# An eighteenth pair of experts' rows in seven products, and the sums added back in two passes instead of four

## What is computed

```
u     = take(expert_down, idx)                    # the picked experts' down rows
act   = gelu(einsum('btd,bthkd->bthk', xi, u))
v_sel = take(expert_up, idx)
out   = einsum('bthk,bthkd->btd', g * act, v_sel)
```

## Time and profile before

| | us |
|---|---|
| median of 3 runs | 2057.95 |
| the runs | 2053.0, 2057.95, 2062.04 |
| profiled execution, its own time | 2054.43 |
| its span, first to last instruction | 2052.6 |
| TensorE busy | 2033.5 (99%), 11770 matmuls |
| VectorE busy | 1644.6 (80%) |
| ScalarE busy | 1360.1 (66%) |
| GpSimd busy | 373.2 (18%) |

### The profile page before, as it was taken

The page is one execution under the profiler, slowest core; times in us unless marked ns, Lnnn a source line. Parts: engine busy times, 40 slices in busy tenths (PEclk is TensorE's granted clock), DMA queues, the critical chain, the costliest instruction groups (busy, mean ns, idle before and its releaser), DMA issues.

```text
span 2052.6 us, 31641 instructions
## 1 busy us (share of the span) xinstructions
PE 2033.5 (99%) x11770; PEld 1748.5 (85%) x11770; DVE 1644.6 (80%) x2959; ACT 1360.1 (66%) x2309; POOL 373.2 (18%) x183
## 2 busy tenths in 40 slices
PE   8999999999999999999999999999999999999998
PEld 7788988888888888887888888888888888888888
DVE  7968988889879999877589888899699999733456
ACT  6664688878756666566646888787566666544674
POOL 1447800000000000012379100000000000045341
PEclk9999999999999999999999999999999999999999
DMA  6445855555566566664357655555556656666454
GB/s 232 154 155 166 237 174 173 170 170 167 173 195 204 187 211 207 205 206 147 125 167 220 193 173 166 174 171 168 184 198 210 200 193 206 214 220 196 128 156 138
DMA packets 108461, 376.26 MB, mean 183 GB/s; under 512 B 12372, under 2 KB 17908, under 8 KB 107412
## 3 DMA queue, kind: packets, MB, share of 16 engines
q1 hardware_dynamic: 107444, 369.00, 56.9%
q0 software_dynamic: 864, 5.24, 1.3%
HBM read 367.87 MB, written 1.08 MB: 180 GB/s over the span
## 4 chain that ended last, share of the span: by engine, by line
PE 95%; DVE 3%; ACT 1%; issue 0%; DMA 0%; POOL 0%; SPq 0%; DVEq 0%; ACTq 0%
PE ps L211 29%; PE ps L205 15%; PE ps L212 15%; PE ps L207 15%; PE ps L206 15%; PE ps L1120 3%; PE ps L1099 1%; DVE arena L813 1%; DVE WL L192 1%; PE ps L1143 0%; DVE arena L810 0%; PE ps L2388 0%; PE ps L2412 0%; PE ps L1146 0%; PE ps L1847 0%
## 5 line engine op out<-in xcount | busy, mean ns | idle before, releaser
L186 ACT ACTIVATE WH<-raw 128x1024 fp32r<-128x1024 f32 (+1 forms) x680 | 700.2, 1035 | 293.7 <-PE ps L207 192.5
L211 PE MATMUL ps<-X,WH 128*128 128x512 f32 x2528 | 893.1, 396 | 0.1
L212 PE MATMUL ps<-X,WL 128*128 128x256 f32 x2528 | 707.6, 280 | 0.0
L192 DVE TENSOR_TENSOR WL<-raw,WH 128x1024 fp32r<-128x1024 f32 (+1 forms) x554 | 659.8, 1193 | 51.7 <-ACT WH L186 51.3
L198 POOL TENSOR_TENSOR WL<-raw,WH 128x1024 fp32r<-128x1024 f32 x126 | 319.0, 2556 | 1563.5 <-ACT WH L186 1561.4
L211 PEld LDWEIGHTS ps<-X,WH 128*128 128x128 f32 x2528 | 473.5, 187 | 104.8 <-issue 0.6
L212 PEld LDWEIGHTS ps<-X,WL 128*128 128x128 f32 x2528 | 477.6, 189 | 0.1
L205 PE MATMUL ps<-WH,X 128*128 128x512 f32 (+1 forms) x774 | 305.9, 395 | 1.5 <-DVE X L414 0.9
L207 PE MATMUL ps<-WH,X 128*128 128x512 f32 (+1 forms) x774 | 301.4, 389 | 0.0
L206 PE MATMUL ps<-WL,X 128*128 128x512 f32 (+1 forms) x774 | 301.3, 389 | 0.0
L205 PEld LDWEIGHTS ps<-WH,X 128*128 128x128 f32 x774 | 145.7, 188 | 34.2 <-issue 2.1
(11 more groups left out here) (354 smaller groups left out, 2630.5 us busy)
## 6 DMA issues: line engine op xcount, KB each, us to landing
raw<-in_l_down_dram SPq DMA_DIRECT2D x256, 512.0 KB, 3.6
raw<-in_l_up_dram SPq DMA_DIRECT2D x256, 512.0 KB, 4.2
raw<-in_l_wq_dram SPq DMA_DIRECT2D x32, 512.0 KB, 3.5
raw<-in_w_qk_dram SPq DMA_DIRECT2D x24, 512.0 KB, 4.2
raw<-in_w_gates_dram SPq DMA_DIRECT2D x24, 512.0 KB, 3.5
raw<-in_l_nat_dram SPq DMA_DIRECT2D x16, 512.0 KB, 3.3
raw<-in_l_wout_dram SPq DMA_DIRECT2D x16, 512.0 KB, 3.5
raw<-in_l_win_dram SPq DMA_DIRECT2D x16, 512.0 KB, 3.8
```

Of the source, the lines that this page charges most:

```text
L186: a.activation(WH[:, i % NW, 0:w], raw[:, i % NW, 0:w], ACT.Copy).then_inc(w_high, 1)
L192: v.tensor_tensor(WL[:, i % NW, 0:w], raw[:, i % NW, 0:w], WH[:, i % NW, 0:w], ALU.subtract).then_inc(w_low_v, 1)
L211: t.matmul(PS[:, bank, :], w[0], X2[:, k, :, :].rearrange("p w t -> p (w t)"), start=first, stop=False)
L212: return t.matmul(PS[:, bank, 0:256], w[1], X2[:, k, 0, :], start=False, stop=last)
```

## The change

`SEVEN` becomes 7, 10, ..., 58: 18 pairs a layer, 36 in all. ScalarE's copy stands in the pass 5, no longer 7, behind the last pair's 2p; the four adds of VectorE stand in two passes, the first two in pass 2p + 6 and the last two in pass 2p + 7, no longer one in each of the passes 2p + 8 to 2p + 11. With the last pair moved from 55 to 58 this puts the copy in pass 121 (was 117) and the adds in the passes 122 and 123 (were 118 to 121). 123 is the last pass of the loop; behind it stand the low part of G of pair 63 and the low weights of the chunks 126 and 127.

```diff
--- before.py
+++ after.py
@@ -147,7 +147,7 @@
         trig_up = sem("trig_up")
 
 
-        SEVEN = tuple(range(7, 56, 3))
+        SEVEN = tuple(range(7, 59, 3))
         IN_SEVEN = {base + 144 + 2 * p + j: (l, m, j)
                     for l, base in enumerate((P0, P1)) for m, p in enumerate(SEVEN) for j in range(2)}
         seven_v, seven_a, seven_done = (sem("seven_" + n) for n in ("sums_low", "high", "products"))
@@ -1363,7 +1363,7 @@
                     a.wait_ge(seven_v, seven_count(l, m, "weights4" if r == 0 else "weights13"))
                     w = slice(2 * r + 2, 2 * r + 4) if r == 0 else slice(0, 2)
                     a.activation(HIGH_T[:, w, :], SUM_T[:, w, :], ACT.Copy).then_inc(seven_a, 1)
-            if c == 2 * SEVEN[-1] + 7:
+            if c == 2 * SEVEN[-1] + 5:
                 a.wait_ge(seven_done, len(SEVEN) * (l + 1))
                 a.activation(SUM_T[:, 0:2, :], PS[:, 0:2, :], ACT.Copy).then_inc(seven_a, 1)
 
@@ -1664,8 +1664,10 @@
                     seven_weights(v, l, p, r + 2)
                 if r in (1, 3):
                     seven_weights_low(v, l, p, r // 2)
-            if 0 <= c - 2 * SEVEN[-1] - 8 < 4:
-                seven_add(v, l, c - 2 * SEVEN[-1] - 8)
+            step = 2 * (c - 2 * SEVEN[-1] - 6)
+            if step in (0, 2):
+                seven_add(v, l, step)
+                seven_add(v, l, step + 1)
 
         def peer_vector(v, l):
             wq, down, up = bases(l)
```

## The result

The change makes the kernel slower: 2065.59 us, median of 9 runs (2062.36 to 2066.5), against 2057.41 of the kernel before on the same chip (9 runs, 2053.0 to 2062.04). The ratio of the runs is 1.0032, with an interval from 1.0021 to 1.0043: **+6.6 us, 4.3 to 8.8**. The forecast was +3.9 and 2060.8 with a range from 2055 to 2066; the time lies inside that, if barely, and the move is under the 0.5% that was called no change.

What follows compares the result with a forecast made beforehand. TensorE, busy 99% of the span, was taken as the bound. A layer's stall of 2.61 us less 0.68 saved gives +1.93, twice +3.9, on a base of 2056.9: 2060.8 us, range 2055 to 2066.

Steps and rivals of the forecast that it cites:

- The saving: Pair 58 takes 21 matmuls instead of 24: 0.68 us less a layer; saving alone as a rival, stall under 0.7 us: 0.13.
- The sums of the eighteenth pair are hidden: VectorE and ScalarE work for pair 58's sums costs nothing; up to 5.2 us for one set if cover failed.
- The adds hold up chunk 126: At a layer's end VectorE's four adds delay chunk 126's low weights, stalling TensorE 2.06 us.
- Second wait and restarts: Chunk 127 starts 0.35 us late, and two TensorE restarts from idle cost 0.10 us each, per layer.
- One of the signs named ahead: Profile after should show two more TensorE waits a layer, about 2.1 and 0.35 us, released by VectorE's L192.
- The end-to-end reading of VectorE: Upper bound: each VectorE instruction starts only when the previous ended, 0.5 us more a layer, 2059.3 on the profile.
- Loads and norm behind the stall: Next stage's weight loads lose 0.7 us of lead, priced at nothing; the norm's chain shifts with TensorE without extra term.
- The rival of late loads: 0.7 us of lost load lead paid at the seam in both layers: +1.4 us, 2062.1; chance inside the stall's 0.80.
- T: Moment the last such pair's sums end on TensorE: start of chunk 115 before, of chunk 121 after the change.
- The clock: Rival: clock halves after the stall between chunks 125 and 126, 36 matmuls cost 8.2 us more a layer, 2077; chance 0.03.
- The base: Mean of three timed runs and the profiled one, 2056.9 us, to which 3.9 was added.
- The expected span of 2056.5: Sign in the profile after: the whole execution's span, 2052.6 us before, would become 2056.5.

Runs made afterwards that it cites:

- e4: Kernel after with the first two adds left in pass 122, the rest behind chunk 127's low weights, the add to X by halves: 2056.93 us, ratio 0.9999.
- e10: e4 with seventeen pairs instead of eighteen, the copy and first two adds kept in passes 121 and 122: 2059.63 us, ratio 1.0006.
- e6: Kernel after without the add of the four banks to the rows X, the last of VectorE's four adds: 2056.65 us, ratio 1.0000.
- e5: Kernel after, unchanged, timed and profiled once more: 2063.7 us, ratio 1.0026.
- e2: Kernel after with seventeen pairs as before, copy still in pass 121 and adds in passes 122 and 123: 2065.16 us, ratio 1.0041.
- e3: Kernel after with seventeen pairs, so the copy is in pass 115 and the adds two to a pass in 116 and 117: 2057.64 us, ratio 1.0001.
- e7: Kernel after with only the first 1024 of 2048 columns of the last add, to the rows X: 2060.07 us, ratio 1.0009.
- e8: Kernel after with one more VectorE operation of 1024 columns behind the last add, into memory nothing reads: 2065.83 us, ratio 1.0040.

## Why the forecast was right in kind and short in size

- *The saving.* 21 instead of 24 matmuls a pair: six fewer on the page. Too small to be timed (e4), and there in the traces, e4 against before and against e10, with 0.6 us a layer or more.
- *The sums of the eighteenth pair are hidden.* Right: e4 and e6 have them and lose nothing. The wait of 0.23 us for a low part of G at 855.17 in the profile after, which with the matmuls around it costs 0.7 us, isn't in e5 or e4.
- *The adds hold up chunk 126.* Right, and the term's first part was sized well: the bracket of 1.96 us is 2.11 us of delay, against 2.06. e2 has the waits without the pair, e3, e4 and e6 the pair or the merging without the waits, e7 and e8 move the wait by -1.07 and +1.13 us as VectorE's chain is moved by half of step 3 and one more operation.
- *Second wait and restarts.* 0.35 was forecast for chunk 127 and 0.20 for two restarts. Where the clock stays up, the distance from 126 to L471 grew by 6.38 - 5.79 = 0.59 us, so 0.55 was right. A layer then costs 2.11 + 0.59 - 0.68 = **+2.02 us; the forecast was +1.93**, and the stretch over 1247 matmuls of layer 1 gives +2.00. One of the signs named ahead is met in part only: the second wait, for 127, stands in one layer of two, in both profiles of the kernel after.
- *The end-to-end reading of VectorE.* Not borne out: the chain took 14.08 us against 14.04, with no room for the 0.5 us a layer that it would have added.
- *Loads and norm behind the stall.* No wait there grew, L408's 0.20 stands against 0.19. The rival of late loads is out. Its sum was a little short: by the forecast's own rows the low weights of 126 are ready 12.91 - 9.14 = 3.8 us later against T, and only those of 127 the 3.3 us that it gives for both.
- *The clock.* **This is the term that was mis-sized.** The forecast left the fall out of its sum and treated it as a rival with a chance of 0.03 and a price of 8.2 us a layer, for 36 matmuls at half speed. The chance was far too low and the price far too high. In the six tails with a wait of 1.96 to 2.24 us (the kernel after, e5, e2) it fell in four; in the two with 3.09 us in both; in the four with 0.17 and 0.89 us (e6, e7) in none. And it came back: the granted clock stood at the lower level for 3.41 us in each of the six, long enough for some eight matmuls 0.43 us apart, not 36. The six distances with a fall are 7.55, 7.95, 7.68, 7.64, 7.38 and 7.66 us, mean 7.64, against 6.37 to 6.41 without, so a fall costs 1.0 to 1.6 us, 1.26 in the mean, not 8.2. Eight matmuls at 0.43 for 0.23 us are 1.6 us, which e5 pays in layer 0; it costs less where the slow matmuls take up the wait for 127 or the one for L408, or where it begins in the idle time (e8, layer 0: 1.0). With four falls in six, a layer costs 2.02 + 0.67 x 1.26 = 2.9 and the kernel 5.7 us, against +6.6 (4.3 to 8.8) and +5.4 (3.3 to 7.4) measured. With the falls that the two profiles have, the sum is 2 x 2.02 + 1.17 = 5.2 us for the first and 2 x 2.02 + 1.57 + 1.30 = 6.9 us for e5; their stretches over 1247 matmuls have 5.9 less the 0.7 of the irregular spot, and 6.9. The evidence weighed against it was an idle of 0.81 us, less than half the one forecast: by e7 an idle of that size indeed does nothing, and says nothing of 2 us. A drop of the clock was one of the forecast's own signs of being wrong; the 40 slices hide it, the stretch from 904 to 908 us shows it.
- *The base.* 2056.9 was taken as the mean of four executions; the nine runs timed beside the kernel after have a median of 2057.4. That explains 0.5 of the 4.8 us between 2060.8 and 2065.6.
- *Luck.* The time fell inside the stated range by 0.4 us, and only because the range had been drawn wide for the spread of the runs; no term of the sum reached that far. The expected span of 2056.5 was missed by 8.2 us, and 5.3 of these are the two stretches of the first expert product that were short in the one profile at hand.

What stays open: by what the clock falls behind one wait of 1.96 us and not behind the next, and why the first expert product takes 314.7 us in one stretch and 317.4 in another.

## What to carry to other kernels

A fixed piece of work that is moved towards the end of a stage must be counted against what is still queued behind it on its own engine: here 4.7 us of adds in front of two chunks that had 1.7 and 0.8 us to spare. Put the operands of the bounding engine first and cut the rest so that its pieces fit the gaps that a chain of dependences leaves anyway (e4). And a wait of TensorE has to be priced with what it can do to the clock: here a wait of 2 us cost about 1.3 us more in four cases out of six.

## What the runs showed of the hardware

- A TensorE idle of 1.96 to 2.24 us in the middle of full work was followed by the 1.2 GHz level in four cases out of six, one of 3.09 us in two of two, one of 0.89 us in none of two. Each fall lasted 3.41 us and cost 1.0 to 1.6 us.
- The fall is not tied to the end of the idle time: in e8, layer 0, it came 0.27 us ahead of it, in the kernel after 0.26 us behind it, in e2 1.9 us behind it, where the engine was already at work again and the first matmul behind the wait still has the 0.50 us that it has where the clock stays up.
- The same program has executions whose spans differ by 5 us (2052.6 and 2057.7) through one stage alone, which takes 314.7 or 317.4 us in a layer. Between single profiles of two kernels, less than that says nothing, unless the stages are compared one by one.
